# A mixture of experts on one Trainium2 core: one-hot gather and scatter in split halves, placed inside the neighbouring expert, and loops over one chunk

## What is computed

```python
def moe_swiglu(h, w_router, b_router, w_gate, w_up, w_down):
    logits = (h @ w_router).astype(F32) + b_router.astype(F32)
    top_logits, top_idx = lax.top_k(logits, TOP_K)
    top_w = jax.nn.softmax(top_logits, axis=-1)
    gates = jnp.sum(jax.nn.one_hot(top_idx, N_EXPERTS, dtype=F32) * top_w[..., None], axis=-2)
    out = jnp.zeros(h.shape, F32)
    for e in range(N_EXPERTS):
        y_e = swiglu(h, w_gate[e], w_up[e], w_down[e]).astype(F32)
        out = out + gates[..., e:e + 1] * y_e
    return out.astype(h.dtype)
```

## Time and profile before

| | before |
|---|---|
| median of the runs | 3115.64 us (3112.84 to 3115.70) |
| the profiled execution | 3112.64 us |
| its span | 3110.8 us |
| PE busy in the span | 2692.7 us, 87% |
| DVE | 1901.5 us, 61% |
| ACT | 1493.2 us, 48% |
| granted clock of PE, mean | 0.925 |
| loaded from memory | 555.99 MB, 180 GB/s over the span |

### The profile page before, as it was taken

One profiled execution on the slowest core, in us unless ns is written; L12 is line 12 of the kernel. 1 busy time (PEld: TensorE's weight loads), 2 busy tenths in 40 slices (PEclk: granted clock), 3 DMA queues, 4 the chain that ended last, 5 costly groups with the idle time before them and its releaser, 6 DMA issues. The chain is left out here.

```text
span 3110.8 us, 38817 instructions
## 1 busy us (share of the span) xinstructions
PE 2692.7 (87%) x14405; PEld 2265.4 (73%) x14406; DVE 1901.5 (61%) x2303; ACT 1493.2 (48%) x1824; POOL 87.7 (3%) x96
## 2 busy tenths in 40 slices
PE   3889876998676869899887988999998989898998
PEld 3779764897475558799855867787787768787877
DVE  2455526455579853444455337796444779797978
ACT  2544425443221134444444337685443768686866
POOL 0000002000021300000010000000000000000000
PEclk9999988999788979899988979999999999999999
DMA  9345511454000144255422417897455789797976
GB/s 244 122 138 189 173 55 68 162 188 127 1 7 1 51 139 149 68 190 186 152 70 82 149 48 275 322 346 263 167 186 176 279 293 366 281 378 273 372 289 223
DMA packets 333382, 563.62 MB, mean 181 GB/s; under 512 B 21977, under 2 KB 126617, under 8 KB 332985
## 3 DMA queue, kind: packets, MB, share of 16 engines
q1 hardware_dynamic: 333112, 560.22, 52.1%
HBM read 555.99 MB, written 4.19 MB: 180 GB/s over the span
## 5 line engine op out<-in xcount | busy, mean ns | idle before, releaser
L1072 DVE TENSOR_TENSOR weights_split<-ring,weights_split 128x1024 fp32r<-128x1024 f32 x676 | 818.9, 1224 | 252.9 <-ACT weights_split L1067 202.0
L1116 PE MATMUL ps<-weights_split,expert_split 128*128 128x512 f32 x3864 | 908.4, 395 | 39.2 <-issue 36.0
L1067 ACT ACTIVATE weights_split<-ring 128x1024 fp32r<-128x1024 f32 x676 | 714.8, 1061 | 338.9 <-PE ps L1116 332.5
L1116 PEld LDWEIGHTS ps<-weights_split,expert_split 128*128 128x128 f32 x3864 | 730.0, 190 | 195.6 <-issue 40.6
L289 DVE TENSOR_TENSOR weights_split<-ring,weights_split 128x2048 fp32r<-128x2048 f32 x182 | 413.5, 2274 | 539.5 <-ACT weights_split L280 539.5
L280 ACT ACTIVATE weights_split<-ring 128x2048 fp32r<-128x2048 f32 x182 | 345.3, 1899 | 505.0 <-PE ps L365 504.6
L365 PE MATMUL ps<-normed_split,weights_split 128*128 128x256 f32 (+1 forms) x4320 | 535.1, 286 | 45.3 <-PEq L342 43.7
L365 PEld LDWEIGHTS ps<-normed_split,weights_split 128*128 128x128 f32 (+1 forms) x4320 | 532.1, 193 | 51.5 <-issue 46.5
L365 PE MATMUL ps<-weights_split,hidden_split 128*128 128x512 f32 x1032 | 242.6, 391 | 4.2 <-DVE hidden_split L522 4.2
L365 PEld LDWEIGHTS ps<-weights_split,hidden_split 128*128 128x128 f32 x1032 | 190.8, 188 | 43.9 <-DVE hidden_split L522 5.9
L365 PE MATMUL ps<-weights_split,normed_split 128*128 128x512 f32 (+1 forms) x816 | 197.0, 402 | 26.0 <-DVE weights_split L289 16.1
(11 more groups left out here) (337 smaller groups left out, 2223.7 us busy)
## 6 DMA issues: line engine op xcount, KB each, us to landing
ring<-moe_w_gate SPq DMA_DIRECT2D x112, 1024.0 KB, 6.2
ring<-moe_w_up SPq DMA_DIRECT2D x112, 1024.0 KB, 6.5
ring<-moe_w_down SPq DMA_DIRECT2D x112, 1024.0 KB, 6.0
ring<-mlp_w_up SPq DMA_DIRECT2D x32, 1024.0 KB, 5.4
ring<-mlp_w_down SPq DMA_DIRECT2D x32, 1024.0 KB, 4.8
ring<-xa_w_kv SPq DMA_DIRECT2D x16, 1024.0 KB, 5.2
ring<-moba_w_qkv SPq DMA_DIRECT2D x12, 1024.0 KB, 11.3
ring<-da_w_qkv SPq DMA_DIRECT2D x12, 1024.0 KB, 5.1
```

The source lines that it names most:

```text
L1067: nc.scalar.activation(split_piece(p, 0), ring_piece(p), ACT.Copy).then_inc(high.sem, 1)
L1072: nc.vector.tensor_tensor(split_piece(p, 1), ring_piece(p), split_piece(p, 0).bitcast(F32), ALU.subtract)\
L1116: last = nc.tensor.matmul(ps[:, banks[half][tt], :], stationary(s, k, tt), split_piece(p, i)[:, kk * NW:(kk + 1) * NW], start=(opens and n ...
```

## The change

- The rows of the tokens (`hn`) are split once into high and low fp32r halves, `hn_split`; `sel` is fp32r. `gather` multiplies both halves, 32 fp32r matmuls of 128 columns into four banks, and `keep_rows` (ACT) copies them: the gathered rows come out split, and DVE's subtraction goes.
- The result of an expert is split too (`y`, high half by ACT, low half by DVE), and `scatter` has eight fp32r matmuls of 512 columns. It runs in the next expert, between its gate and up products; the first expert scatters zeros, and the last one's scatter stands behind the loop. DVE adds the tiles to `x` (`add_scattered`) behind its ninth weight piece of that expert.
- The next expert's selection is made behind the first chunk's round, and its gather runs ahead of the last four pieces of down products.
- The pieces of an expert are cut into an opening of 8 (gate and up of chunk 0), six rounds of 12 (gate, turn, up, down) and the last four. Rounds 2 to 6 are one inner loop on each engine. Gate, up, turn and hidden rows have one bank or buffer each instead of two; in a round ACT copies the turned rows behind its fifth piece and DVE subtracts behind its sixth.
- The dense form is cut into rounds in the same way; its additions release the next gather.
- The router's weights are split and stationary, 24 fp32r matmuls of 256 columns; the bias is added by ACT, and the logits are turned. The router's steps on DVE are reordered, the gates behind the first selection.
- `x` is stored tile by tile, each when its last addition is done.
- `arena`, `toep` and `weights_split` are freed ahead of the mixture and placed anew, to make room for `hn_split` and `y`.

Cut to what the argument speaks of:

```diff
+        e.wait_ge(*wr_low.at(1))
+        for k in range(KD):
+            for n, (i, j) in enumerate(PASSES):
+                last = nc.tensor.matmul(ps[0:NE, 0, 0:T], wr_split[:, i, k, :], core.XS[:, j, k, :],
+                                        start=(k + n == 0), stop=(k == KD - 1 and n == 2))
+        last.then_inc(*logits.up())
...
+        for tt in range(TT):
+            e.wait_ge(*hn_high.at(tt + 1))
+            nc.vector.tensor_tensor(hn_split[:, 1, tt, :], hn[:, tt, :], hn_split[:, 0, tt, :].bitcast(F32), ALU.subtract)\
+                .then_inc(*hn_low.up())
...
+        nc.vector.memset(y.rearrange("p i d -> p (i d)").bitcast(F32), 0.0)
+        nc.vector.memset(selT.bitcast(F32), 0.0)
...
-        for k in range(KD):
-            for tt in range(TT):
-                last = nc.tensor.matmul(ps[:, 6 + k // 4, k % 4 * CAP:(k % 4 + 1) * CAP], hn[:, tt, k * P:(k + 1) * P],
-                                        sel[:, tt, :], start=(tt == 0), stop=(tt == TT - 1))
-            if k % 4 == 3:
-                last.then_inc(gathered.sem, 1)
...
+        for i in range(2):
+            for k in range(KD):
+                for tt in range(TT):
+                    last = nc.tensor.matmul(ps[:, GATHER_BANKS[2 * i + k // 4], k % 4 * CAP:(k % 4 + 1) * CAP],
+                                            hn_split[:, i, tt, k * P:(k + 1) * P], sel[:, tt, :],
+                                            start=(tt == 0), stop=(tt == TT - 1))
+                if k % 4 == 3:
+                    last.then_inc(gathered.sem, 1)
+
+    def keep_rows(act, e):
+
+        for b in range(4):
+            act.wait_ge(gathered.sem, e * 4 + (b + 1))
+            nc.scalar.activation(XG[:, b // 2, b % 2 * NW:(b % 2 + 1) * NW], ps[:, GATHER_BANKS[b], :], ACT.Copy)\
+                .then_inc(xg_kept.sem, 1)
+
+    def scatter(pe, e):
+
+        pe.wait_ge(y_high.sem, e + 1)
+        pe.wait_ge(y_low.sem, e + 1)
         for tt in range(TT):
-            last = nc.tensor.transpose(ps[:, 5, tt * P:(tt + 1) * P], sel[:, tt, :], c("ident"))
+            for half in range(2):
+                for i in range(2):
+                    last = nc.tensor.matmul(ps[:, (6, 2)[tt] + half, :], selT[:, tt * P:(tt + 1) * P],
+                                            y[:, i, half * NW:(half + 1) * NW], start=(i == 0), stop=(i == 1))
+            last.then_inc(scattered.sem, 1)
...
+    def add_scattered(dve, e):
+
+        dve.wait_ge(y_low.sem, e + 1)
+        dve.wait_ge(summed.sem, e * TT)
+        for tt in range(TT):
+            dve.wait_ge(scattered.sem, e * TT + (tt + 1))
+            add_tile(dve, e, tt, (6, 2)[tt]).then_inc(summed.sem, 1)
...
+    def slots_round_pe(pe, u, opens):
+        pe.wait_ge(silud.sem, u + 1)
+        products(pe, u, OPENING, [[GATE]] * 2, rows, True, True)
+        slots_turn(pe, u)
+        products(pe, u, OPENING + 4, [[UP]] * 2, rows, True, True)
+        pe.wait_ge(ht_split.sem, u + 1)
+        products(pe, u, OPENING + 8, [[DOWN[0]], [DOWN[1]]], hidden, opens, False, down=True)
...
+        u0 = ex * N
+        pe.wait_ge(xg_kept.sem, ex * 4 + 4)
+        products(pe, u0, 0, [[GATE]] * 2, rows, True, True)
+        scatter(pe, ex)
+        products(pe, u0, 4, [[UP]] * 2, rows, True, True)
+        pe.wait_ge(summed.sem, ex * TT + TT)
+        turn_selection(pe, ex)
+        slots_round_pe(pe, u0, True)
+        with pe.Fori(1, N - 1) as r:
+            slots_round_pe(pe, pe.snap(ex * N + r), False)
+        slots_turn(pe, u0 + (N - 1))
+        pe.wait_ge(silud.sem, u0 + N)
+        pe.wait_ge(sel_kept.sem, ex + 1)
         gather(pe, ex + 1)
...
+        products(pe, u0, pieces - 4, [[DOWN[0]], [DOWN[1]]], hidden, False, True, down=True)
...
+    def slots_round_act(act, u):
+        for i in range(ROUND):
+            high_half(act, u, OPENING + i + AHEAD)
+            if i == 3:
+                slots_silu(act, u, OPENING + i, u + 1)
+            if i == 4:
+                slots_hidden_high(act, u)
...
+        with act.Fori(1, N - 1) as r:
+            slots_round_act(act, act.snap(ex * N + r))
+        slots_hidden_high(act, u0 + (N - 1))
+        keep_rows(act, ex + 1)
+        for p in range(pieces - 4, pieces):
+            high_half(act, u0, p + AHEAD)
+        consumed(act, u0, pieces - 1)
+        nc.scalar.activation(y[:, 0, :], ps[:, DOWN[0]:DOWN[0] + 2, :].rearrange("p b n -> p (b n)"), ACT.Copy)\
+            .then_inc(y_high.sem, 1)
...
+    def slots_round_dve(dve, u):
+        for i in range(ROUND):
+            low_half(dve, u, OPENING + i + AHEAD)
+            if i == 5:
+                slots_hidden_low(dve, u)
+            if i == 7:
+                slots_gate(dve, u, OPENING + i, u + 1)
...
+        u0 = ex * N
+        for p in range(OPENING):
+            low_half(dve, u0, p + AHEAD)
+            if p == 4:
+                add_scattered(dve, ex)
+            if p == 7:
+                slots_gate(dve, u0, p, u0)
+        slots_round_dve(dve, u0)
         dve.wait_ge(sel_turned.sem, ex + 1)
         select(ex + 1)
-        keep_low(dve, ex + 1)
+        with dve.Fori(1, N - 1) as r:
+            slots_round_dve(dve, dve.snap(ex * N + r))
+        slots_hidden_low(dve, u0 + (N - 1))
+        for p in range(pieces - 4, pieces):
+            low_half(dve, u0, p + AHEAD)
+        dve.wait_ge(y_high.sem, ex + 2)
+        nc.vector.tensor_tensor(y[:, 1, :], ps[:, DOWN[0]:DOWN[0] + 2, :].rearrange("p b n -> p (b n)"),
+                                y[:, 0, :].bitcast(F32), ALU.subtract).then_inc(y_low.sem, 1)
```

More of the change, by code:

```diff
@@ L1106, in products, with turn_selection, keep_selection @@
+    def turn_selection(pe, e):
+        for tt in range(TT):
+            last = nc.tensor.transpose(ps[:, 7, tt * P:(tt + 1) * P], sel[:, tt, :].bitcast(F32), c("ident"))
+        last.then_inc(sel_turned.sem, 1)
+    def keep_selection(act, e):
+        act.wait_ge(sel_turned.sem, e + 1)
+        nc.scalar.activation(selT, ps[:, 7, 0:T], ACT.Copy).then_inc(sel_kept.sem, 1)
+    def products(pe, u, p0, banks, stationary, opens, closes, down=False):
         tts = len(banks[0])
-        for half in parts:
-            j = EXPERT_TILES.index((part, chunk, half))
+        for half in range(2):
@@ L1256, in dense_act @@
-    def dense_act(act, ex):
-        for p in range(pieces):
-            high_half(act, ex, p + AHEAD)
-            for chunk in range(N):
-                if p == last_of["gate", chunk]:
-                    act.wait_ge(used.sem, used_value(ex, p))
-                    for tt in range(TT):
-                        last = nc.scalar.activation(tmp[:, tt, :], ps[:, tt, :], ACT.Silu)
-                    last.then_inc(silud.sem, 1)
-                if p == (last_of["down", chunk - 1] if chunk else last_of["up", 0]):
-                    act.wait_ge(turned.sem, ex * N + (chunk + 1))
-                    nc.scalar.activation(HT[:, 0, :], ps[:, 2:4, :].rearrange("p b n -> p (b n)"), ACT.Copy)\
-                        .then_inc(ht_high.sem, 1)
-        act.sem_inc(y_kept.sem, 1)
-        keep_high(act, ex + 1)
@@ new lines, in dense_pe @@
+    def dense_pe(pe, ex):
+        u0 = ex * N
+        pe.wait_ge(xg_kept.sem, ex * 4 + 4)
+        scatter(pe, ex)
+        pe.wait_ge(summed.sem, ex * TT + TT)
+        turn_selection(pe, ex)
+        products(pe, u0, 0, [[0, 1]] * 2, all_rows, True, True)
+        products(pe, u0, 4, [[2, 3]] * 2, all_rows, True, True)
+        dense_turn(pe, u0)
+        pe.wait_ge(sel_kept.sem, ex + 1)
+        dense_round_pe(pe, u0, True)
+        with pe.Fori(1, N - 1) as r:
+            dense_round_pe(pe, pe.snap(ex * N + r), False)
+        pe.wait_ge(ht_split.sem, u0 + N)
+        products(pe, u0, pieces - 4, DENSE_DOWN, all_hidden, False, True, down=True)
+        pe.wait_ge(y_low.sem, ex + 2)
+        gather(pe, ex + 1)
```

425 lines of the change are left out of this document (220 added, 205 removed).

## The result

| | changed kernel |
|---|---|
| median of the runs | 3072.35 us (3069.78 to 3074.03, four runs); beside it the kernel before 3114.24 us |
| ratio to before | 0.9865, 95% interval 0.9848 to 0.9882 |
| the profiled execution | 3069.78 us, span 3068.0 us (forecast 3059.3 and 3057.5) |
| expert on slots, turn of the selection to the next one | 128.9 us (forecast 129.0) |

A forecast was written before the change was run, and what follows sets the result against it. PE's products bound the mixture, with 19.7 us between experts on waits, f32 gather and scatter, branches and clock. 1879 + 7 x 129.0 + 264.6 + 10.9 = 3057.5 us of span, 3062 as run median; range 3040 to 3112.

The forecast's parts named there:

- Head: Before the first expert: router 5.3 us instead of 13.13, partly given back on DVE; first product at 1879 instead of 1881.37.
- Experts on slots: Seven of eight experts: 129.0 us each against 137.4, with the clock staying at 1.00.
- Gather: Slots boundary: 32 fp32r matmuls at 0.124 us, 4.0 us; bounds 2.0 and 7.3 us.
- additions: Slots expert: PE waits 1.0 us (0 to 2.5) for DVE's two additions to x before turning the selection.
- rounds: Slots expert: PE waits 0.64 us for the hidden rows' low half in each of 6 chunks, 3.8 us.
- The dense expert: The one expert of eight in dense form: enter 7.6, products 247.5, leave 9.5; 264.6 us (260 to 272) against 281.1.
- Tail: Last product to the end: 10.9 us against 18.4, from y, scatter, additions and storing the second half MB.
- Branches: Expert loop and If on PE: both taken as hits, 0.5 us an expert; inner-loop branches on PE, ACT, DVE cost nothing.
- Rival A: Expert's branches on PE still miss, 7 boundaries x 6.8 = 48 us: 3110 us; chance 0.17.
- Rival B: Inner-loop branch stalls on DVE, 2.3 us in each of 35 rounds: 3152 us; chance 0.13 with its table-load relative.
- Rival C: Gather costs the 512-column price, or half the branches miss: 3086 to 3088 us; chance 0.15.
- Rival D: Hidden rows are in time in the slots rounds, 27 us less: 3035 us; chance 0.08 for it and below.

The follow-up runs named there:

- e10: Changed kernel with the inner rounds of both forms written out on ACT and DVE alone, PE keeping its loops: 3113.47 us.
- e9: Changed kernel with the inner rounds of both forms written out on PE alone, ACT and DVE keeping their loops: 3079.52 us.
- e6: Changed kernel with ACT's high and DVE's low half of the hidden rows one weight piece earlier in each slots round: 3043.31 us.
- e1: Changed kernel with the slots form's inner rounds written out on PE, ACT and DVE, the dense form keeping its loop: 3090.41 us.
- e4: Changed kernel with the next expert's gather and ACT's copies of it behind the last down products on slots instead of ahead: 3099.14 us.

## Why the prediction was right or wrong

Range, sign and size held. By its steps, in the span (forecast in brackets): first product at 1874.85 (1879), two experts on slots 260.6 (258.0), the dense one 274.6 (264.6), five on slots 646.0 (645.0), tail 11.9 (10.9): 3068.0 (3057.5).

*Head, 4.1 us better.* The rows of the chain:

```profile
1865.67 7.08 PE ps L1117 x32
1874.85 8.65 PE ps L1177 x24
```

and of PE's timeline:

```profile
1847.98 5.29 PE L999 MATMUL ps<-normed_split,rows_split 128*8 128x256 f32 x24 [4.04 <-DVE rows_split L1018]
```

The router's 24 records took 5.3 us, as forecast. They ended at 1853.27, some 2 us ahead of what I had counted: they began 1.2 us earlier than the old router, where I had allowed 1.0 us more for splitting the weights. The way from there to the first product took 21.6 us, some 2 us less than I had counted. The gather is slow here (7.08 us) and so are the first products (8.65 for 24): the granted clock is 0.70 from 1865 to 1892, which my 258.0 left out, +2.6.

*Experts on slots, right to 0.2 us at full clock.* Gather 3.61 (4.0), scatter 1.81 (1.8), additions 1.10 (1.0), rounds 6 x 0.72 = 4.3 (3.8), branches nothing on the path (0.5). The width of the gather's matmuls did not matter, as the two forms of the earlier trace rows had said: 0.113 us for 128 columns.

*The dense expert, the term that was mis-sized,* 10.0 us; that this is also nearly the whole miss of 10.5 is chance, since the head's -4.1 cancels the +4.6 of the slots and the tail. PE, around its entry and its end:

```profile
2139.12 2.59 PE L1137 MATMUL ps<-rows_split 128*128 128x512 f32 x8 [3.63 <-DVE rows_split L1301]
2143.55 24.35 PE L1177 MATMUL ps<-weights_split,normed_split 128*128 128x512 f32 x96
2171.50 1.97 PE L1315 MATMUL ps<-const,arena 128*128 128x128 f32 x8 [3.60 <-DVE arena L1384]
...
2402.05 7.09 PE L1117 MATMUL ps<-rows_split 128*128 128x128 f32 x32 [7.21 <-DVE residual L1143]
2410.10 7.31 PE L1177 MATMUL ps<-weights_split,expert_split 128*128 128x512 f32 x24 [0.96 <-ACT expert_split L1127]
```

and DVE at the end, behind the last product at 2394.84:

```profile
2395.97 1.23 DVE L1102 TENSOR_TENSOR weights_split<-ring,weights_split 128x1024 fp32r<-128x1024 f32 x1 [1.49 <-ACT weights_split L1097]
2397.12 0.48 DVE L980 TENSOR_SCALAR rows_split<-const,arena 128x128 fp32r<-128x128 f32 x2
2397.97 1.76 DVE L1414 MEMSET rows_split<- 128x2048 f32 x1 [0.38 <-issue]
2399.65 2.35 DVE L1143 SCALAR_TENSOR_TENSOR residual<-ps,small,residual 128x1024 f32<-128x1024 f32 x2
```

Entering took 8.1 us (7.6). The products took 251.3 (247.5): the first 96 ran in 24.35 us where the old kernel's took 22.67, at a granted clock of 0.83 from 2130 to 2150. The 3.60 us ahead of the first turn stood in the old kernel too. Leaving took 15.3 (9.5): I put 2.8 us of additions ahead of the gather, and DVE had the last weight piece, the selection and the clearing of y (1.76 us) there first, 7.2 us; the gather behind that wait took 7.09 us and not 4.0. The 2.0 us for branches were not needed: a branch of 3.57 us is recorded at 2405.1, but beside the gather. I had taken the slots form's gather place as if it held for both forms.

*Tail.* PE's last scatter:

```profile
3059.75 3.75 PE L1137 MATMUL ps<-rows_split 128*128 128x512 f32 x8 [3.63 <-DVE rows_split L1301]
```

3.63 us of wait for y as forecast; the scatter at the lower clock had its first half ready for DVE 2.2 us after its start, not 1.1.

*The cause of the gain was named only in part.* The step that failed is "Branches": it looked at PE's branch records alone, called them the largest unknown, and had no term for ACT's and DVE's branches but the inner loops' nothing. PE's did fall to 0.21 us, as forecast. But the loops are what the gain hangs on, and in the new order those of ACT and DVE are worth 41 us (e10) and those of PE 7 (e9). The forecast's time needed ACT and DVE to be quick at their branches too, and it had not looked at them. Rival A's price, 3110 against 3113.5, came by luck: it is 7 x 6.8 us of PE's own branches, which took 0.21. Rival B's stall at DVE's inner branch didn't come: after the first expert no packet moves on q14, and a round lasts 17.53 us (the records' 56 ns prove nothing, since a stall stands behind them). Nor did table loads in the rounds: there are 7 for the weight pieces and 7 for Silu, one each for an expert on slots. Rival C's half gain didn't come. Rival D is e6: 27 us was forecast for it, 29.0 was measured.

What stays open: why PE's branches missed at every boundary of the old kernel and only at two in e9, whose path on PE is about as long; the count of instruction packets (73 on q8 from the mixture's start in the old kernel, 26 in e9) says that the old code was fetched anew in each expert, not why. No run changed the old kernel, where PE's idle time at a boundary (4.06 us) stood behind its own branches: how its loss was shared between PE's branches and ACT's and DVE's is not shown. Nor is it whether ACT or DVE alone would do the harm.

## What to carry to other kernels

A long loop body can stall every engine that runs it, and what counts is the one whose work is due soonest behind the branch: look for idle time without a releaser behind the branch on ACT and DVE, not only at PE's branch records. On ACT and DVE the form that is jumped over counted too; an inner loop in either form was enough. When a step is moved into another's shadow, cost its place in each form that the code has (the rare one too), and give the step a buffer or a queue place such that no wait is created in the inner rounds: 0.72 us there undid 30 us. A wait of about 3 us on PE can cost twice its length, since the clock may fall behind it.

## What was not expected of the hardware

- ACT's branch records stay at 45 ns when the target must be fetched; the 6.95 us stood in no record. PE's carry the stall (up to 6.1 us) in themselves.
- PE's misses pass: in the profiled executions of e1 and e9 PE missed at the end of the dense expert and at the next boundary, and then not again.
- The same 2.75 us of idle time let the clock fall at one boundary of e4 and not at the next.
- ACT and DVE stalled at every boundary with both forms written out (40.3 us in e10) and at no slots boundary with the slots form alone written out (1.1 us in e1), on the same path.
- Removing a wait recorded as 0.43 us shortened the round by 0.72.
